# Sixteen thousand experts and a second block: 128 tokens by fetched rows, four raw weight places, a group norm inside another scan

## The reference, cut to what matters

```
def peer(xn, w_query, sub_keys, u_tab, v_tab):       # 8 heads, 16 experts a head: 128 experts a token
    ...                                              # idx: which of 16384 experts, g: their weights
    u = u_tab[idx]
    a = gelu(einsum('chkd,cd->chk', u, xc))          # dot product of a token with each chosen row of u
    vv = v_tab[idx]
    return einsum('chk,chkd->cd', g * a, vv)         # weighted sum of the chosen rows of v

# second block's mixer, for y (512 wide: 8 heads of 64) out of the RWKV scan
    mu, var = mean(y), mean(square(y - mu))          # over each head's 64 channels
    y = (y - mu) * rsqrt(var + RWKV_GN_EPS) * ln_w + ln_b
    y = (y + bonus) * g                              # RWKV's half of the mixer's output
    o = gla_chunked(q, k, v, log_a)                  # GLA, both directions: chunks of 64 tokens, a state in between
    o = rms_norm(o, norm_w) * silu(gate)             # GLA's half
    ...
    y = concatenate([y_rwkv, y_gla]) @ w_out
```

## Time and profile before

| | us |
|---|---|
| median of 3 runs | 2885.52 (2877.62 to 2885.55) |
| profiled execution, its time | 2883.86 |
| profiled execution, span of the instructions | 2882.1 |
| PE busy, of the span | 93% |
| DVE, ACT, POOL busy | 59%, 38%, 32% |
| 16 DMA engines, mean | 166 GB/s |

### The profile page before, as it was taken

The page is one execution under the profiler, slowest core; times in us unless marked ns, Lnnn a source line. Parts: engine busy times, 40 slices in busy tenths (PEclk is TensorE's granted clock), DMA queues, the critical chain, the costliest instruction groups (busy, mean ns, idle before and its releaser), DMA issues. The chain is left out here.

```text
span 2882.1 us, 48320 instructions
## 1 busy us (share of the span) xinstructions
PE 2669.0 (93%) x18416; PEld 2371.8 (82%) x18416; DVE 1686.4 (59%) x2920; ACT 1091.5 (38%) x1757; POOL 913.4 (32%) x622
## 2 busy tenths in 40 slices
PE   6999989999999999799999999699799788999996
PEld 5766768999999999799999999567699675887775
DVE  1354349986887887556766667437566645333115
ACT  3366333444333333233333333354334454333223
POOL 2622333565121122311111111133444232444442
PEclk9999999999999999999999999799899999999998
DMA  3211222455788788978888888224822001333331
GB/s 120 92 59 52 81 94 80 118 163 174 253 279 295 250 274 305 333 228 294 300 293 290 300 293 280 93 81 147 262 58 52 17 23 59 95 99 97 103 95 66
DMA packets 200994, 478.89 MB, mean 166 GB/s; under 512 B 58368, under 2 KB 107648, under 8 KB 199552
## 3 DMA queue, kind: packets, MB, share of 16 engines
q1 hardware_dynamic: 173184, 375.93, 40.7%
q0 software_dynamic: 27648, 100.68, 9.8%
HBM read 405.23 MB, written 71.30 MB: 165 GB/s over the span
## 5 line engine op out<-in xcount | busy, mean ns | idle before, releaser
L152 ACT ACTIVATE weights_high<-weights_raw 128x1024 fp32r<-128x1024 f32 x433 | 458.7, 1060 | 1384.9 <-PE psum L260 1199.9
L160 POOL TENSOR_TENSOR weights_low<-weights_raw,weights_high 128x1024 fp32r<-128x1024 f32 x219 | 550.1, 2512 | 828.0 <-ACT weights_high L152 827.9
L258 PE MATMUL psum<-expert_in_high,weights_high 128*128 128x416 f32 (+1 forms) x1152 | 424.1, 368 | 26.9 <-DVE weights_low L160 14.8
L259 PE MATMUL psum<-expert_in_low,weights_high 128*128 128x416 f32 (+1 forms) x1152 | 413.6, 359 | 0.0
L260 PE MATMUL psum<-expert_in_high,weights_low 128*128 128x416 f32 (+1 forms) x1152 | 412.6, 358 | 0.0
L258 PE MATMUL psum<-coefficients_high,weights_high 128*128 128x416 f32 x1024 | 364.9, 356 | 15.4 <-DVE weights_low L160 10.5
L259 PE MATMUL psum<-coefficients_low,weights_high 128*128 128x416 f32 x1024 | 361.0, 353 | 0.0
L260 PE MATMUL psum<-coefficients_high,weights_low 128*128 128x416 f32 x1024 | 360.8, 352 | 0.0
L160 DVE TENSOR_TENSOR weights_low<-weights_raw,weights_high 128x1024 fp32r<-128x1024 f32 x214 | 262.1, 1225 | 96.8 <-ACT weights_high L152 96.7
L258 PEld LDWEIGHTS psum<-expert_in_high,weights_high 128*128 128x128 f32 x1152 | 219.2, 190 | 43.5 <-ACT expert_activation L1163 16.9
L1391 POOL DMA_INDIRECT expert_rows<-in_weights,row_numbers x96 | 97.4, 1015 | 480.5 <-DVE s_by_token_then_row_sums L1431 414.2
(11 more groups left out here) (398 smaller groups left out, 5103.2 us busy)
## 6 DMA issues: line engine op xcount, KB each, us to landing
weights_raw<-in_weights SPq DMA_DIRECT2D x435, 512.0 KB, 3.9
expert_activations<-expert_activation SPq DMA_DIRECT2D x128, 208.0 KB, 5.0
coefficient_table<-table_stage SPq DMA_DIRECT2D x8, 3328.0 KB, 13.6
table_group<-coefficient_table SPq DMA_DIRECT2D x128, 208.0 KB, 4.7
activation_in<-expert_activations SPq DMA_DIRECT2D x128, 208.0 KB, 5.3
a_and_kk_then_chunks<-scan_vectors SPq DMA_DIRECT2D x8, 768.0 KB, 6.4
scan_vectors<-scan_stage SPq DMA_DIRECT2D x4, 1280.0 KB, 7.3
scan_vectors<-scan_stage SPq DMA_DIRECT2D x4, 1024.0 KB, 6.2
```

The costliest lines, as they stand in the source:

```text
L152: act.activation(d.hi[:, m % SPLIT, :], d.raw[:, m % RAW, :], ACT.Copy).then_inc(d.high, 1)
L160: pool.tensor_tensor(d.lo[:, m % SPLIT, :], d.raw[:, m % RAW, :], d.hi[:, m % SPLIT, :].bitcast(F32), ALU.subtract).then_inc(d.split, 1)
L258: pe.matmul(acc, w[0][:, cols], x[0], start=start, stop=False)
L259: pe.matmul(acc, w[0][:, cols], x[1], start=False, stop=False)
```

## The change

- `GT` goes from 96 to 128: 128 tokens by fetched rows, 384 by dense products (416 before), in blocks of 48 (52 before). The second group of `Rows` is now 64 tokens wide, so there are 128 fetches from each table.
- The dot products: five in four tiles of the table stage (one a tile before), the remaining 38 evenly over END's 16 tiles (24 in its first 12 before).
- `RAW` goes from 2 to 4. The loops over the first 40 up tiles are written as 2 x 20 on SP, POOL and ACT (the count must be a multiple of `RAW`); PE's loop is as before.
- `rwkv_output` is gone. Its work is in a class `RwkvOutput`, whose parts stand between the steps of `gla_scan`; the gate's Silu is at the end of ACT's part.
- The scratch memory for the descriptors of POOL's DMAs is set to 8192 bytes a partition.

```
-RAW = 2
+RAW = 4
-GT = 96
+GT = 128
-TB = 52
+TB = 48
...
-                with act.Fori(0, ex.CH) as i:
-                    for j in range(ex.CHS):
-                        up(i, ex.CHS, j, j)
-                        if j == ex.CHS // 2 + 1:
-                            pick.scalar_exp(act, i)
-                    pick.scalar(act, i)
+                with act.Fori(0, ex.CH // 2) as i:
+                    for j in range(2 * ex.CHS):
+                        up(i, 2 * ex.CHS, j, j)
+                        if j % ex.CHS == ex.CHS // 2 + 1:
+                            pick.scalar_exp(act, i * 2 + j // ex.CHS)
+                        if j % ex.CHS == ex.CHS - 1:
+                            pick.scalar(act, i * 2 + j // ex.CHS)
...
-                            rows.dot(dve, j)
+                            for s in range(5 * j // 4, 5 * (j + 1) // 4):
+                                rows.dot(dve, s)
...
-                    for s in range(dots + 2 * j, min(dots + 2 * j + 2, rows.N)):
+                    for s in range(dots + (rows.N - dots) * j // ex.END, dots + (rows.N - dots) * (j + 1) // ex.END):
...
-    GROUPS = ((0, 64), (64, 32))
+    GROUPS = ((0, 64), (64, 64))
...
-            rwkv_output(nc, k, dram, gate, bonus, ys, gg)
...
+class RwkvOutput:
+    BANKS = (2, 3, 6, 7)
...
+    def banks_free(self, pe, g):
+        pe.wait_ge(self.lnd, 2 * g + 2)
...
 # gla_scan, gpsimd: each half of bd is cleared ahead of its first use
+                    if i < 2:
+                        if i:
+                            for g in range(2):
+                                pool.wait_ge(built[g], 4)
+                        pool.memset(bd[:, i, :, :, :], 0.0).then_inc(zeroed, 1)
...
 # gla_scan, tensor
-                pe.wait_ge(zeroed, 2)
+                rwkv.means(pe)
                 for g in range(2):
                     front(0, g)
+                rwkv.variances(pe)
                 for i in range(NCH):
                     for g in range(2):
+                        if i == 0:
+                            rwkv.banks_free(pe, g)
                         back(i, g)
...
 # gla_scan, scalar
+                rwkv.squares(act)
+                rwkv.logs(act)
                 for i in range(NCH):
                     for g in range(2):
                         o_out(i, g)
                         if i + 1 < NCH:
                             turned(i + 1, g)
+                        rwkv.roots(act, 2 * i + g)
+                act.wait_ge(gate_in, 16)
+                act.activation(gg[:, :, :], gg[:, :, :], ACT.Silu)
...
 # gla_scan, vector
-                dve.wait_ge(zeroed, 2)
+                rwkv.sum_directions(dve)
+                dve.memset(pb[:, :, :], 0.0).then_inc(cleared, 1)
+                rwkv.centre(dve)
+                dve.wait_ge(cleared, 1)
...
                         state(i, g)
                         masks(i + 1, g)
+                        rwkv.finish(dve, 2 * i + g)
...
+    nc = bacc.Bacc("TRN2", target_bir_lowering=False, num_devices=1, dynamic_dma_scratch_size=8192)
```

## The result

The changed kernel takes 2851.64 us, median of 5 runs (2847.86 to 2860.0), against 2885.52 (2877.62 to 2886.88, 5 runs) before: a ratio of 0.9892 [0.9876, 0.9909]. It is faster by about 34 us (31 by the ratio), where 87 was forecast. The profiled execution took 2853.3.

The account below looks back on a forecast made before the run. PE was taken to bound the first 40 tiles, table stage and down, transfers END. -12.8 - 30.7 + 13 - 46 - 10.5 = -87 us gave 2798 us, range 2765 to 2845.

Parts of the forecast that it names:

- Down, -46: Down stage: 116 tiles at 4.28 us and twelve without rows at 4.18 take 546.6 us, 46 less.
- The transfers' floor of 4.28: Down: us a tile that transfers allow, taken between 4.17 by bytes and 4.34 by engine time.
- rival C: Down's transfers cannot exceed END's average 328 GB/s: 4.56 us a tile, down -14, END +21, total 2838; chance 0.24.
- the 0.14 a tile: Down: us a tile lost before the change (4.63 against PE's 4.49), taken as hidden by four raw places.
- a down pace over 4.4: Down: a sign, set beforehand, that the forecast is wrong; us a tile, where 4.28 was forecast.
- Rival B: Transfers never bind outside END: down at 4.17 us a tile (-59), total 2769; chance 0.18.
- Table stage, -30.7: Table stage: cheaper matmuls save 23.0 us and eight fewer table steps 7.7, so it takes 400 us.
- Raw places elsewhere 0: Outside END and down: ACT's other eight waits for raw weights, 43 us, priced at 0 within 5 us.
- END, +13: END: bound by transfers, 38 dot products instead of 24 make it 108 us, 13 more.
- First 40 tiles, -12.8: First 40 up tiles: 0.32 us less PE time in each, 12.8 us in all.
- GLA, -10.5: Group norm inside the GLA scan: -13 to the first `back`, +3 for Silu; taken as -10.5 us.
- The descriptors' scratch: Scratch for fetch descriptors: priced at 0; if it paced fetches, END could be 42 us over its forecast value.

Follow-up runs that it names:

- order4: The changed kernel with SP issuing down's raw-weight loads two iterations later, so loads queued behind that wait go out earlier: 2782.14 us, ratio 0.9658.
- before_ar8: The kernel before the change with eight places for `activation_in` instead of four, nothing else: 2869.81 us, ratio 0.9941.
- rows96: The changed kernel with 96 tokens by fetched rows and the earlier dot products again, four raw places and new GLA scan kept: 2870.37 us, ratio 0.9967.
- rows96_ar8g2: rows96 with eight places for `activation_in` and the `table_group` loads two tiles earlier: 2855.74 us, ratio 0.9925.
- ar8g2: The changed kernel with eight places for `activation_in` instead of four and the `table_group` loads two tiles earlier: 2788.68 us, ratio 0.966.
- raw2: The changed kernel with two places for raw weights instead of four: 2878.25 us, ratio 0.9999.

## Why the prediction was wrong

**Down, -46, measured 0: the step that failed.** The matmul's price was right: tiles of 4.16 (4.17). The transfers' floor of 4.28, and rival C's 4.56, were not needed: with nothing late, all of it comes at PE's pace. The 4.34 by engine time had taken the share as fixed for each byte, and it isn't: 294 GB/s at 0.87 in the earlier trace rows make 338 at a full share, 353 at 0.97 in order4 make 364. What failed is the sentence "Four raw places hide the start of late weights; that is why I don't add the 0.14 a tile which down loses now." It took the 0.14 x 128 = 18 us for ACT's waits in the earlier trace rows. before_ar8 shows them to be the late loads of `activation_in` and what follows from them: eight places for it, and two for raw weights, take 18.4 us off down. I had read ACT's waits and not DVE's, which has the longer ones in the same stage.

And the loss doesn't stay 18 us. The late loads set a pace of their own, by the loop above, and PE's work isn't in it: 9.7 us for two tiles before, 9.9 after, while PE's need for them fell from 8.98 to 8.32. Over late and punctual loads together, two tiles took 9.35 us before and 9.47 after. With four raw places in both kernels the lateness cost 588.2 - 574.5 = 13.7 us with 416 columns (rows96, rows96_ar8g2) and 593.0 - 529.5 = 63.5 with 384 (after, ar8g2). The growth of 49.8 eats the 45.0 that the rows are worth (rows96_ar8g2 to ar8g2) and the 4.5 of the raw places. So the step took down to be bound by PE or by the rate of transfers, and it was bound by one load's way from issue to use. The forecast's own test, "a down pace over 4.4", caught it: 4.63.

**Rival C** gives 2838, the nearest number, for a wrong reason: no rate held it. Rival B's mechanism, transfers that never bind in down, is what order4 shows once they are issued in time. The Trainium skill's "DMA: Bandwidth & Descriptors" has the 358 GB/s of the prediction in Specifications, but says under Bandwidth that this holds with both cores of the memory's domain streaming, and lists more for one alone. This kernel uses one core, and ar8g2's 365 GB/s over 70 us are over 358: I had taken a limit that doesn't bind here.

**Table stage, -30.7, measured -38.5,** 96 steps cost 0.89 each now (pitches of 5.05 and 4.16), not 0.96, which is 6.7 of the difference; and the sum held only since raw weights were in time. "Raw places elsewhere 0" is wrong: without them the stage takes 414.4. PE's 426.5 of 431.1 in the earlier trace rows showed that such waits cost nothing at the old pace, and nothing of the new one.

**END, +13, measured +14.3:** right in size, share 0.96 at 350 GB/s, but not in place, so in part luck: the window that I priced grew by 3.8 us only (95.1 to 98.8), and 10.5 came in the tail up to the first coefficient (1.9 to 12.4), where DVE still does dot products (the last starts at 1204.7). Not all of it is rate: the 14.8 us behind the twelve loads are again a queue, and of the fetches taken out of END in ar8g2 the first nine were worth 2.1 us each and the next nine 0.5, not 1.47.

**First 40 tiles, -12.8, measured -1.7.** The sum took only PE's work. At the old pace DVE's picks came in time; now PE is 4.6 us early once, and the wait is followed by the half clock. Together they cost some 7 us at that tile (13.17 against 6.02 in raw2), but taking the wait away gave back only 2.9 to 4.0: then more waits for POOL's lows show, and the stage stays at 174.4.

**GLA, -10.5, measured -7.1** from the start of the group norm to the end. The 9.7 to 11.3 us to the first `back` were 13.2, by means at half clock (granted 0.50 from 2253.9 to 2260.7) and squares behind the turned copies; Silu's +3 was right, and the finish pieces fit.

The rest of the sum: the stages start 0.9 us earlier, and 3.0 us more pass between down and the group norm. -0.9 - 1.7 - 38.5 + 14.3 + 0.3 + 3.0 - 7.1 = -30.6, the difference of the spans. The 3.0 are within what that stretch varies by from one execution to the next. The descriptors' scratch was priced at 0: order4 has it and keeps PE busy for 480 of 480 us in down, so it holds nothing back there; no run tests it in END.

## What to carry over

Before you price a faster engine, list for its stage every transfer that anything waits for, on each engine, with the time from its issue to its need, and follow what its issue waits for. Where that leads back to the transfer's own user, it is a loop, and if the loop takes as long as the tiles it spans, a faster engine outside it gains nothing. An in-order queue that issues loads is a place where a wait for one buffer delays the loads of all others: put each wait where its own condition comes true, and here a ring of four did what eight did. A rate below the limit beside an idle PE can mean that nobody asked in time, and not that the path is full; down was such a case (315 GB/s, then 353).

## What was not expected of the hardware

With nothing late, the mix of down, small rows and fetches among it, ran at 353 to 355 GB/s for 480 us and at 365 for 70, about the 359 that the earlier trace rows had in END. Moving one wait in SP's queue did this without a byte, a buffer or an instruction more in any tile.
